# Keys of the streams and states of the matrix memory turned by VectorE from 128-byte pieces

## The chip, the cores and the metric

One core of one Trainium2 chip runs the whole kernel. The metric is the device time in microseconds, as the median of several runs. In the profile PE is TensorE, DVE VectorE, ACT ScalarE, POOL GpSimd and SP SyncE; PEld is TensorE's weight load, SPq the queue in which SP issues DMAs.

## The reference, cut to what matters

The kernel computes one layer for two groups of rows: 16 meta tokens with 256 new frames (the prompt), and 16 new frames of each of 8 running streams. One projection gives queries, keys and values of a differential attention (4 heads, two key halves of 128) and of an mLSTM matrix memory (4 heads), whose outputs are joined, projected, and followed by an MLP of 8192 columns. Two inputs have the wrong axis inside for TensorE: the cached keys and the stored states.

```python
def diff_attn_block(q, k, v, ...):            # k: cached keys of the last 256 frames, then the new ones
    s = jnp.einsum('bqhcd,bkhcd->bchqk', q, k) * (DQK_ATT ** -0.5) + bias
    p = jax.nn.softmax(s, axis=-1)
    w = p[:, 0] - lam * p[:, 1]
    o = jnp.einsum('bhqk,bkhd->bqhd', w, v)
    return rms_norm(o, subln_g) * (1.0 - lam_init)

def step(carry, blkin):                       # mLSTM, C: (streams, heads, 256, 128)
    num = einsum('bhts,bshe->bthe', A, vb) + iw * jnp.einsum('bhed,bthd->bthe', C, qb)
    ...
    C_new = dec * C + jnp.einsum('bhs,bshe,bshd->bhed', sw, vb, kb)
```

## The kernel before

All products are in float32. A weight matrix is read in pairs of tiles; a tile (2048 x 128, or 512 x 512 for the output projections) has four quarters. SP loads half a tile, 512 KB, at a time into one of four slots of raw (load_tile, load_rows, L462 and L469); ScalarE rounds a quarter to w_hi (split_hi, L481), VectorE takes the rest w_lo (split_lo, L490), and TensorE multiplies w_hi with the high and the low part of the activations and w_lo with the high part (mm_tile L510 to L512, mm_out L555 to L557). There are four buffers of split quarters; ScalarE waits until TensorE has done with the quarter four before. A slot of raw is loaded again when VectorE has split it.

The attention and the matrix memory are worked in beside these weight products. After every quarter each engine takes what is due from a list written out in advance: ATT_PLAN over tiles 24 to 41 (slot 0 is the first quarter of tile 24) and HEAD_PLAN over tiles 42 to 55. Each engine runs its items in order, between its own parts of the weight work, and waits on semaphores for what it needs from the others. TensorE takes slot n behind quarter n of the stage; VectorE takes slot n behind its split of the quarter four further on.

ATT_PLAN has 16 steps, the 8 streams and 8 blocks of the prompt in turn, one in four slots. For a stream the cached keys (256 frames x 1024, 1 MB) are loaded by POOL into kc, one buffer, when TensorE has turned those of the stream before. In slots -4 and -2 from the stream's scores TensorE transposes them with 16 products against the identity (turn, L1793) into PSUM, and ScalarE (L979) and VectorE (L1459) copy a half of each to kT, which has the feature in the partition and the frame inside. scores reads kT. In slot 1 of the stage VectorE also adds the mask to the bias (L1448).

HEAD_PLAN has 13 slots per head, the first head at slot 2: rows and decay at 0, scores, exponentials and weighted keys at 1, states at 2, weigh at 3, cn (products of the new state) at 4, take0 to take3 (new_state, L1603: decays C_rows and adds the products) from 4 to 6, num at 6, and then the norm, the gate and the turned output. The states of a head for all streams, 1 MB, are loaded by POOL into C_rows, which has the value's row in the partition (load_C). states turns them with 16 products into PSUM, and ScalarE copies them to C_T (L1064), which num reads. C_rows is then updated in place, stored by POOL as C_sample, and loaded with the next head.

Queues: SP issues the weight loads, and behind those of tile t the spill of tile t - 3 (the rows of mv and mo that the matrix memory needs later, L804), and from tile 50 on four loads of the residual (load_x, L811 and L812). POOL issues in one order: kc and vc of the streams; then mvo (the spilled rows; for one head it waits for that head's spills) and for each head the store of C_rows, the store of the prompt's state, the load of C_rows for the next head, and mvo of the head after that. ScalarE issues the stores of new keys (ko).

Of the kernel before, what the change touches and what calls it, by code (L numbers as in the profile page):

```python
# [19 lines left out]
P = 128  # L20
D = 2048
KT = D // P
# [38 lines left out]
T_OUT2 = 56  # L61
T_MLP = 64
# [54 lines left out]
KEYS_AT = (-4, -2)  # L117
# [3 lines left out]
HEAD_AT = (("rows", 0), ("decay", 0), ("scores", 1), ("expo", 1), ("ksw", 1), ("states", 2), ("weigh", 3), ("cn", 4),  # L121
           ("take0", 4), ("take1", 5), ("take2", 5), ("take3", 6), ("num", 6), ("hsum", 6), ("cp", 7), ("og", 7),
           ("hroot", 8), ("hturn", 11), ("gate", 11))
EXPO_LATE, EXPO_TAIL = 3 * P, 5 * P
DVX = DV + 2
# [80 lines left out]
def plan_banks():  # L206
# [20 lines left out]
    for _, what, n in ATT_PLAN:  # L227
        if what == "av":
            u.add(("av", n), (2, 4)[n % 2])
        elif what == "ko":  # L230
            u.add(("ko", n), 4)
        elif what == "keys":
            for i in range(2):
                u.add(("kT", n[0], 2 * n[1] + i), i)
        elif what == "scores":
            u.add(("s", STEPS[n], 0), 2)
            u.add(("s", STEPS[n], 1), 3)
        elif what == "turn":
            u.add(("w", STEPS[n]), 4)
        elif what == "out":  # L240
            u.add(("o", STEPS[n]), 5)
        elif what == "oturn":
            u.add(("oT", STEPS[n]), 1)
    u.add("nT", 1)
    for _, what, h in HEAD_PLAN:
# [7 lines left out]
        elif what == "states":  # L253
            for i in range(4):
                u.add(("ct", h, i), i % 3)
# [16 lines left out]
def build(nc, x_prompt, x_sample, cache_k, cache_v, state_C, state_n, state_m, meta_tokens, rel_bias, norm1_g,  # L272
# [6 lines left out]
    with ctx:  # L279
# [45 lines left out]
        ocol = sb("ocol", [P, 2, 6])  # L325
        n_sq = sb("n_sq", [P, 2, TOK])
        n_y = sb("n_y", [P, 2, TOK])
        n_t = sb("n_t", [P, TOK])
        g1 = sb("g1", [P, KT])
        g1_rows = sb("g1_rows", [KT, P])  # L330
# [30 lines left out]
        with ExitStack() as s:  # L361
            kc = sb("kc", [P, 2, ATTW], scope=s)
# [93 lines left out]
        def load_tile(e, pair, j, w, krow, col):  # L456
            for half in range(2):
# [4 lines left out]
                e.dma_start(raw[:, slot], w_source(w, krow + half * 8 * P, col)).then_inc(raw_landed[slot], 16)  # L462

        def load_rows(e, pair, j, w, krow, col):
            for half in range(2):
# [4 lines left out]
                            src.rearrange("(k p) n -> p k n", p=P)).then_inc(raw_landed[slot], 16)  # L470

# [156 lines left out]
        def _(e):  # L628
# [46 lines left out]
            dma(kc[:], cache_k[0, 0].rearrange("(a p) h n -> p a (h n)", p=P), "kc_in")  # L675
# [26 lines left out]
            for b in range(1, BD):  # L702
                done(e, ("kT", b - 1, 3))
                dma(kc[:], cache_k[0, b].rearrange("(a p) h n -> p a (h n)", p=P), "kc_in")
                if b >= 2:
                    done(e, ("o", b - 2))
                    dma(vc[:, b % 2], cache_v[0, b].rearrange("(a p) h n -> p a (h n)", p=P), f"vc_in{b % 2}")
# [72 lines left out]
        def _(e):  # L780
# [33 lines left out]

            for t in range(T_M, T_OUT):
                col = (N_MQ, N_MQ + 8 * P, N_MO)[(t - T_M) // 8] + P * ((t - T_M) % 8)
                load_tile(e, t // 2, t % 2, w_in[0], 0, col)
                spill(t - 3)
            for t in range(T_OUT, T_MLP):
                half, c = out_at(t)  # L820
                load_rows(e, t // 2, t % 2, w_out[0], (8 * half + 4 * (t % 2)) * P, 4 * c * P)
# [21 lines left out]
        def _(e):  # L843
# [108 lines left out]
            def att_work():  # L952

                for slot, what, n in ATT_PLAN:
                    yield slot
                    step = STEPS[n] if what in ("exp", "turn", *OUT_STEPS) else None
                    if what == "ko":

                        b = take(e, ("ko", n))
                        if n == 0:  # L960

                            e.wait_ge(S("kc_in"), 16)
# [11 lines left out]
                    elif what == "keys":  # L974
                        i = 2 * n[1]
                        k = take(e, ("kT", n[0], i))
                        if n[0]:
                            done(e, ("s", n[0] - 1, 1))
                        taken(e.activation(kT[:, 2 * i:2 * i + 2].rearrange("p c k -> p (c k)"), k[:], ACT.Copy),  # L979
                              ("kT", n[0], i))  # L980
# [55 lines left out]
            def head_work():  # L1036
                for slot, what, h in HEAD_PLAN:
                    yield slot
                    vo = None if what == "take" else mvo[:, h % 2]
# [21 lines left out]
                    elif what == "states":  # L1061
                        for i in range(4):
                            b = take(e, ("ct", h, i))
                            ins = e.activation(C_T[:, 2 * i:2 * i + 2, 0:DV], b[:].rearrange("p (s d) -> p s d", d=DV),  # L1064
                                               ACT.Copy)
                            taken(ins, ("ct", h, i))
# [67 lines left out]
            e.wait_ge(S("n_stored"), 32)  # L1134
            for t in range(T_OUT2, T_MLP):
# [46 lines left out]
        def _(e):  # L1182
# [253 lines left out]
            def att_work():  # L1436

                for slot, what, n in ATT_PLAN:
# [15 lines left out]
                    elif what == "keys":  # L1454
                        i = 2 * n[1] + 1
                        k = take(e, ("kT", n[0], i))
                        if n[0]:
                            done(e, ("s", n[0] - 1, 1))
                        taken(e.tensor_copy(kT[:, 2 * i:2 * i + 2].rearrange("p c k -> p (c k)"), k[:]),  # L1459
                              ("kT", n[0], i))  # L1460
# [135 lines left out]

            def new_state(h, i):

                b = take(e, ("cn", h, i))
                for half in range(2):  # L1600
# [35 lines left out]
            def head_work():  # L1636
                for slot, what, h in HEAD_PLAN:
                    yield slot
                    vo = None if what == "take" else mvo[:, h % 2]
# [23 lines left out]
                    elif what == "take":  # L1663
                        new_state(*h)
                    elif what == "cp":
# [118 lines left out]
        def _(e):  # L1784
# [163 lines left out]
            def att_work():  # L1948
                for slot, what, n in ATT_PLAN:
# [7 lines left out]
                    elif what == "keys":  # L1957
                        b, part = n
                        e.wait_ge(S("kc_in"), 16 * (b + 1))
                        for i in (2 * part, 2 * part + 1):  # L1960
                            turn(("kT", b, i), [(x * P, kc[:, x % 2, (2 * i + x // 2) * P:(2 * i + x // 2 + 1) * P])
                                                for x in range(4)])
# [16 lines left out]
            def numerators(h):  # L1979
                read_out(e, ("vn0", h), ("vn1", h), ("sx", h), ("sy", h), *[("ct", h, i) for i in range(4)])  # L1980
# [45 lines left out]
            def head_work():  # L2026
                for slot, what, h in HEAD_PLAN:
# [19 lines left out]
                    elif what == "states":  # L2047

                        e.wait_ge(S("C_in"), 32 * (h + 1))
                        for i in range(4):  # L2050
                            turn(("ct", h, i), [(x * P, C_rows[:, (4 * i + x) // 2, x % 2]) for x in range(4)])
# [135 lines left out]
```

## Time and profile before

| | |
|---|---|
| median of 3 runs | 1790.0 us (1789.85 to 1791.39) |
| the profiled execution | 1790.15 us, its span 1788.3 us |
| granted clock of TensorE | 1.00 |
| busy: PE, PEld | 1779.4, 1616.8 us |
| busy: DVE, ACT, POOL | 878.0, 694.5, 137.9 us |
| DMA | 251.42 MB, 141 GB/s in the mean |

The times in the profile are counted from the start of the span. The attention stage lies between about 243 and 465 us, the head stage between about 467 and 637 us. Products are pipelined: a row gives how long one product lasts, and the distance of two starts is what it costs in a sequence.

### The profile page before, as it was taken

The page shows a single profiled execution, that of the slowest core. Times are in us where ns is not written, and L with a number is a line of the kernel's source. Part 1 is how long each engine was busy: PE and PEld are TensorE (multiplying, and loading weights), DVE is VectorE, ACT ScalarE, POOL GpSimd, SP SyncE. Part 2 cuts the span into 40 slices and gives each one's busy share as a digit, 9 for nine tenths or more (in the row PEclk, how much of TensorE's full clock was granted, in tenths as well). Part 3 has the DMA queues.
Part 4 walks back from the last instruction along what each step waited for, and adds up shares of the span by engine and source line. Part 5 has one row for each costly group of instructions (what it writes and reads, how often), then busy time and mean ns, then how long its engine had stood idle before and what let it go on. Part 6 is the DMA issues. An engine that isn't in the chain of part 4 may idle for free.

```text
span 1788.3 us, 27850 instructions
## 1 busy us (share of the span) xinstructions
PE 1779.4 (100%) x9702; PEld 1616.8 (90%) x9702; DVE 878.0 (49%) x1678; ACT 694.5 (39%) x1320; POOL 137.9 (8%) x183
## 2 busy tenths in 40 slices
PE   9999999999999999999999999999999999999999
PEld 8999998999998888999888999888999888999887
DVE  5634774555566645555334444334445334445333
ACT  5324754544445444333323333323333332333332
POOL 3300000000111100111000111000111000111000
PEclk9999999999999999999999999999999999999999
DMA  7754456565666533444344444344443343443442
GB/s 193 224 142 108 107 156 207 149 193 144 192 183 222 159 120 120 119 125 128 121 128 129 119 127 123 125 129 126 120 129 119 127 129 121 125 126 120 147 147 95
DMA packets 297426, 251.42 MB, mean 141 GB/s; under 512 B 9340, under 2 KB 244156, under 8 KB 297356
## 3 DMA queue, kind: packets, MB, share of 16 engines
q1 hardware_dynamic: 281446, 209.50, 40.1%
q0 software_dynamic: 11088, 37.18, 6.2%
q10 hardware_dynamic: 4822, 3.80, 0.7%
q8 instruction: 46, 0.75, 0.2%
q14 instruction: 24, 0.20, 0.0%
HBM read 234.87 MB, written 15.56 MB: 140 GB/s over the span
## 4 chain that ended last, share of the span: by engine, by line
PE 97%; DVE 1%; DMA 1%; ACT 1%; issue 0%; POOL 0%; ACTq 0%; DVEq 0%
PE acc L510 18%; PE acc L511 17%; PE acc L512 17%; PE bank L597 8%; PE bank L598 8%; PE bank L596 8%; PE bank L1786 3%; PE ssb L596 2%; PE ssb L597 2%; PE ssb L598 2%; PE bank L1793 1%; PE ssb L1786 1%; PE bank L556 1%; PE bank L557 1%; PE bank L555 1%; PE acc L555 1%
## 5 line engine op out<-in xcount | busy, mean ns | idle before, releaser
L490 DVE TENSOR_TENSOR w_lo<-raw,w_hi 128x512 fp32r<-128x512 f32 x768 | 557.7, 734 | 829.0 <-ACT w_hi L481 828.3
L481 ACT ACTIVATE w_hi<-raw 128x512 fp32r<-128x512 f32 x768 | 482.7, 630 | 857.8 <-PE acc L512 425.0
L511 PE MATMUL acc<-x2g_lo,w_hi 128*128 128x384 f32 x1024 | 348.0, 340 | 0.0
L510 PE MATMUL acc<-x2g_hi,w_hi 128*128 128x384 f32 x1024 | 345.8, 338 | 0.0
L512 PE MATMUL acc<-x2g_hi,w_lo 128*128 128x384 f32 x1024 | 344.6, 337 | 0.0
L510 PE MATMUL acc<-a_hi,w_hi 128*128 128x400 f32 (+1 forms) x768 | 268.9, 350 | 0.2 <-DVE w_lo L490 0.2
L511 PE MATMUL acc<-a_lo,w_hi 128*128 128x400 f32 (+1 forms) x768 | 262.7, 342 | 0.0
L512 PE MATMUL acc<-a_hi,w_lo 128*128 128x400 f32 (+1 forms) x768 | 262.4, 342 | 0.0
L597 PE MATMUL bank<-w_lo,a_hi 128*128 128x512 f32 x640 | 253.0, 395 | 0.0
L598 PE MATMUL bank<-w_hi,a_lo 128*128 128x512 f32 x640 | 252.6, 395 | 0.0
L596 PE MATMUL bank<-w_hi,a_hi 128*128 128x512 f32 x640 | 252.0, 394 | 0.0
L512 PEld LDWEIGHTS acc<-x2g_hi,w_lo 128*128 128x128 f32 x1024 | 193.4, 189 | 0.0
L511 PEld LDWEIGHTS acc<-x2g_lo,w_hi 128*128 128x128 f32 x1024 | 192.3, 188 | 0.2
L510 PEld LDWEIGHTS acc<-x2g_hi,w_hi 128*128 128x128 f32 x1024 | 191.9, 187 | 0.5 <-DVE w_lo L490 0.3
L510 PEld LDWEIGHTS acc<-a_hi,w_hi 128*128 128x128 f32 x768 | 144.2, 188 | 3.1 <-issue 1.7
L598 PEld LDWEIGHTS bank<-w_hi,a_lo 128*128 128x128 f32 x640 | 120.7, 189 | 27.7
L597 PEld LDWEIGHTS bank<-w_lo,a_hi 128*128 128x128 f32 x640 | 120.3, 188 | 27.8
L596 PEld LDWEIGHTS bank<-w_hi,a_hi 128*128 128x128 f32 x640 | 120.4, 188 | 27.6
L512 PEld LDWEIGHTS acc<-a_hi,w_lo 128*128 128x128 f32 x768 | 144.7, 188 | 0.0
L511 PEld LDWEIGHTS acc<-a_lo,w_hi 128*128 128x128 f32 x768 | 144.4, 188 | 0.2
L762 POOL TENSOR_TENSOR a_lo<-n_sq,a_hi 128x384 f32 x64 | 64.9, 1015 | 959.8 <-ACT a_hi L1155 959.8
L1155 ACT ACTIVATE a_hi<-n_sq 128x384 f32 (+1 forms) x64 | 33.7, 526 | 131.9 <-DVE n_sq L1744 131.9
(340 smaller groups left out, 1529.0 us busy)
## 6 DMA issues: line engine op xcount, KB each, us to landing
raw<-in_w_up SPq DMA_DIRECT2D x128, 512.0 KB, 4.0
raw<-in_w_down SPq DMA_DIRECT2D x128, 512.0 KB, 3.9
raw<-in_w_in SPq DMA_DIRECT2D x94, 512.0 KB, 4.1
raw<-in_w_out SPq DMA_DIRECT2D x32, 512.0 KB, 3.9
kc<-in_cache_k POOLq DMA_DIRECT2D x8, 1024.0 KB, 6.6
vc<-in_cache_v POOLq DMA_DIRECT2D x8, 1024.0 KB, 9.1
C_rows<-in_state_C POOLq DMA_DIRECT2D x8, 512.0 KB, 8.0
out<-C_rows POOLq DMA_DIRECT2D x8, 512.0 KB, 5.2
```

The lines of the kernel that those rows point to most:

```text
L481: e.activation(w_hi[:, q], raw[:, slot, 4 * (q % 2):4 * (q % 2) + 4, :], ACT.Copy).then_inc(hi_ready, 1)
L490: e.tensor_tensor(w_lo[:, q], raw[:, slot, 4 * (q % 2):4 * (q % 2) + 4, :], w_hi[:, q].bitcast(F32), ALU.subtract).then_inc(lo_ready, 1)
L510: e.matmul(out, w_hi[:, q, kk], hi[:, k, at], start=k == 0, stop=False, skip_group_check=True)
L511: e.matmul(out, w_hi[:, q, kk], lo[:, k, at], start=False, stop=False, skip_group_check=True)
L512: last = e.matmul(out, w_lo[:, q, kk], hi[:, k, at], start=False, stop=k == KT - 1, skip_group_check=True)
L555: e.matmul(out, a_hi[:, k, rows], hi_w, start=k % 8 == 0, stop=False, skip_group_check=True)
L596: e.matmul(out, a_hi[:, k, rows], hi_w, start=k == 0, stop=False, skip_group_check=True)
L597: e.matmul(out, a_hi[:, k, rows], lo_w, start=False, stop=False, skip_group_check=True)
L598: last = e.matmul(out, a_lo[:, k, rows], hi_w, start=False, stop=k == KT - 1, skip_group_check=True)
L762: e.tensor_tensor(a_lo[:, bass.ds(2 * i + j, 1), LIVE], n_sq[:, j:j + 1, LIVE], a_hi[:, bass.ds(2 * i + j, 1), LIVE].bitcast(F32), ALU.sub ...
L1155: e.activation(a_hi[:, at, LIVE], n_sq[:, j:j + 1, LIVE], ACT.Copy).then_inc(S("u_hi_made"), 1)
L1786: return e.matmul(out, lhsT, rhs, start=start, stop=stop, skip_group_check=True)
```

## The change

The cached keys are no longer loaded by POOL as whole frames. SP loads them in four parts per stream into kc (now 128 x 4 x 512), each part with four DMAs of 32 partitions, whose pieces are 32 features (128 bytes): partition 32j + r holds the features 32j to 32j + 31 of frames 8r to 8r + 7. Parts 0 and 1 are issued behind the first half, parts 2 and 3 behind the second half of the weight loads of tiles 25, 27, ... 39. A part is loaded when the same part of the stream before has been turned. VectorE turns each part with one transpose of 128x512, which transposes every block of 32 x 32 and writes a frame's element 8 places behind the last, in slots -4, -3, -2 and -1 from the scores.

The states are loaded twice: by POOL into C_rows as before (now waited for by VectorE in take0), and by SP into a new buffer C_blk in 128-byte pieces, 4 parts of 8 DMAs per head, all 32 issued in one go behind the second half of the weight loads of tiles 41, 46, 49 and 52 (STATE_LOADS), ahead of that tile's spill. VectorE turns them with four such transposes per head, in slots -2, -1, 1 and 2 from the head's start, right into C_T. C_blk lies in the memory of n_sq, n_y and n_t, which are free in these stages.

The 192 transposing products of kc and C_rows, their banks and the copies L979, L1459 and L1064 are gone. POOL's loads of vc no longer have the loads of kc between them.

```diff
+STATE_LOADS = (41, 46, 49, 52)
-KEYS_AT = (-4, -2)
+BLOCKS_AT = (-4, -3, -2, -1)
+STATES_AT = (-2, -1, 1, 2)
...
-            plan += [(s + KEYS_AT[0], "keys", (step, 0)), (s + KEYS_AT[1], "keys", (step, 1))]
+            plan += [(s + at, "key_blocks", (step, i)) for i, at in enumerate(BLOCKS_AT)]
...
+        plan += [(s + at, "state_blocks", (h, i)) for i, at in enumerate(STATES_AT)]
...
+            def load_keys(b, i):
+                if b:
+                    e.wait_ge(S("blocks_turned"), 4 * (b - 1) + i + 1)
+                for j in range(4):
+                    e.dma_start(kc[32 * j:32 * j + 32, i].rearrange("p (x d) -> p x d", d=32),
+                                bass.AP(tensor=cache_k.tensor, offset=(b * PAST + 2 * i) * ATTW + 32 * j,
+                                        ap=[[8 * ATTW, 32], [P, 16], [1, 32]])).then_inc(S(f"kc_in{i}"), 16)
+            def load_states(h, i):
+                if h:
+                    e.wait_ge(S("states_turned"), 4 * (h - 1) + i + 1)
+                for x in range(2):
+                    for j in range(4):
+                        e.dma_start(C_blk[32 * j:32 * j + 32, i, x * DV:(x + 1) * DV].rearrange("p (a d) -> p a d", d=32),
+                                    bass.AP(tensor=state_C.tensor, offset=((2 * i + x) * NH + h) * DV * DQ + 32 * j,
+                                            ap=[[8 * DQ, 32], [DQ, 8], [1, 32]])).then_inc(S(f"C_blk_in{i}"), 16)
+            def behind_load(t):
+                if t in STATE_LOADS:
+                    h = STATE_LOADS.index(t)
+                    return lambda half: half and [load_states(h, i) for i in range(4)]
+                b, late = divmod(t - T_M - 1, 2)
+                if b in range(BD) and not late:
+                    return lambda half: [load_keys(b, 2 * half + i) for i in range(2)]
...
+                    elif what == "key_blocks":
+                        b, i = n
+                        e.wait_ge(S(f"kc_in{i}"), 64 * (b + 1))
+                        ...
+                        e.transpose(kT[:].rearrange("p c (r x) -> p x c r", x=8)[:, 2 * i:2 * i + 2],
+                                    kc[:, i].rearrange("p (x c d) -> p x c d", x=2, d=32)).then_inc(S("blocks_turned"), 1)
...
+            def state_blocks(h, i):
+                e.wait_ge(S(f"C_blk_in{i}"), 128 * (h + 1))
+                ...
+                e.transpose(C_T[:, 2 * i:2 * i + 2, 0:DV].rearrange("p b (r a) -> p b a r", a=8),
+                            C_blk[:, i].rearrange("p (b a d) -> p b a d", b=2, d=32)).then_inc(S("states_turned"), 1)
             def new_state(h, i):
                 b = take(e, ("cn", h, i))
+                if i == 0:
+                    e.wait_ge(S("C_in"), 32 * (h + 1))
...
             def scores(n, b):
                 if is_stream(b):
-                    read_out(e, *[("kT", b, i) for i in range(4)])
+                    e.wait_ge(S("blocks_turned"), 4 * b + 4)
```

## Rows read from the trace of the kernel before

**Rows 1.** The page, chain that ended last: shares of the span by engine.
```profile
PE 97%; DVE 1%; DMA 1%; ACT 1%; issue 0%; POOL 0%; ACTq 0%; DVEq 0%
```

**Rows 2.** Timeline of TensorE: start us, us, engine, line, operation, names, count [idle before].
```profile
244.93 1.04 PE L1793 MATMUL bank<-ident,kc 128*128 128x128 f32 x8
245.73 0.42 PE L510 MATMUL acc<-a_hi,w_hi 128*128 128x384 f32 x1
```

**Rows 3.** Timeline of TensorE: the two key groups that waited.
```profile
251.49 0.65 PE L1793 MATMUL bank<-ident,kc 128*128 128x128 f32 x4 [0.46 <-DVE kT L1459]
...
270.86 1.09 PE L1793 MATMUL bank<-ident,kc 128*128 128x128 f32 x8 [1.10 <-DMA kc<-in_cache_k]
```

**Rows 4.** Timeline of TensorE: the states of head 0.
```profile
480.58 2.08 PE L1793 MATMUL bank<-ident,C_rows 128*128 128x128 f32 x16
482.42 0.42 PE L510 MATMUL acc<-a_hi,w_hi 128*128 128x384 f32 x1
```

**Rows 5.** Instructions of kT, VectorE's copies: ns min/median/max, first and last start.
```profile
L1459 DVE COPY kT<-bank x16: 669/683/684, 250.8 to 431.4; 128x512 f32<-128x512 f32 x16
```

**Rows 6.** Stretches: us, then busy us (x) of PE, PEld, DVE, ACT, POOL, PEclk, DMA share, GB/s.
```profile
820.00:836.00 16.00, 16.00 (x92) 16.00 (x92) 8.51 (x12) 5.57 (x10) 2.03 (x2) 1.00 0.40 116
850.00:880.00 30.00, 30.00 (x131) 24.38 (x130) 10.49 (x17) 8.84 (x14) 0.00 (x0) 1.00 0.37 123
...
319.40:345.00 25.60, 25.60 (x194) 23.42 (x193) 12.95 (x41) 12.97 (x40) 1.39 (x2) 1.00 0.60 181
...
550.00:590.00 40.00, 39.48 (x225) 32.11 (x224) 27.00 (x79) 19.37 (x43) 5.67 (x7) 1.00 0.76 251
```

**Rows 7.** Timeline of VectorE at the start of the attention stage.
```profile
252.24 2.29 DVE L1448 TENSOR_TENSOR bias_p<-bias_p,s_sb 128x144 f32<-128x144 f32 x8
...
255.17 0.68 DVE L1459 COPY kT<-bank 128x512 f32<-128x512 f32 x1
...
256.37 0.55 DVE L1234 TENSOR_TENSOR m<-acc,rstd_x 128x384 f32<-128x384 f32 x1
```

**Rows 8.** Timeline of TensorE: first scores of stream 0.
```profile
256.75 0.66 PE L1786 MATMUL bank<-kT,zt 128*32 128x256 f32 x8
```

**Rows 9.** Timeline of VectorE: the splits around the weighing of head 0.
```profile
481.50 0.69 DVE L490 TENSOR_TENSOR w_lo<-raw,w_hi 128x512 fp32r<-128x512 f32 x1 [0.46 <-ACT w_hi L481]
485.52 0.69 DVE L490 TENSOR_TENSOR w_lo<-raw,w_hi 128x512 fp32r<-128x512 f32 x1 [3.32 <-ACT w_hi L481]
```

**Rows 10.** Timeline of SP's queue, tiles 46 and 47.
```profile
492.22 0.52 SPq L804 DMA_DIRECT2D mv_mo<-stage  x1
499.75 8.21 SPq L462 DMA_DIRECT2D raw<-in_w_in  x2
```

**Rows 11.** The page, DMA issues: engine, count, KB each, median us to landing.
```profile
raw<-in_w_in SPq DMA_DIRECT2D x94, 512.0 KB, 4.1
```

**Rows 12.** Instructions of mv_mo, the spills' issues: ns min/median/max, first and last start.
```profile
L804 SPq DMA_DIRECT2D mv_mo<-stage x16: 411/519/3384, 359.1 to 546.2; - x16
```

**Rows 13.** Timeline of ScalarE, VectorE and TensorE: when transfers and splits are wanted.
```profile
517.44 0.63 ACT L481 ACTIVATE w_hi<-raw 128x512 fp32r<-128x512 f32 x1 [1.43 <-PE acc L512]
...
528.65 1.11 DVE L1603 SCALAR_TENSOR_TENSOR C_rows<-C_rows,iwB,bank 128x128 f32<-128x128 f32 x4
...
549.04 1.29 DVE L490 TENSOR_TENSOR w_lo<-raw,w_hi 128x512 fp32r<-128x512 f32 x2 [1.79 <-ACT w_hi L481]
...
552.51 0.40 PE L555 MATMUL acc<-w_hi,a_hi 128*128 128x512 f32 x1
```

**Rows 14.** Timeline of POOL's DMA issues behind head 0.
```profile
497.80 0.70 POOL L630 DMA_DIRECT2D mvo<-mv_mo  x1 [17.37 <-issue]
498.49 1.80 POOL L630 DMA_DIRECT2D out<-C_rows  x2
...
507.94 1.77 POOL L630 DMA_DIRECT2D C_rows<-in_state_C  x2 [6.00 <-DMA out<-C_rows]
```

**Rows 15.** Instructions of C_rows: its products; its DMAs from issue to landing.
```profile
L1793 PE MATMUL bank<-ident,C_rows x64: 270/272/329, 480.6 to 603.2; 128*128 128x128 f32 x64
...
DMA to landing us min/median/max: 3.9/6.0/10.5
```

More of the change, by code:

```diff
@@ L325, in build @@
         ocol = sb("ocol", [P, 2, 6])
+        with ExitStack() as s:
+            C_blk = sb("C_blk", [P, 4, 2 * DV], scope=s)
         n_sq = sb("n_sq", [P, 2, TOK])
@@ L462, in load_tile, with load_rows @@
                 e.dma_start(raw[:, slot], w_source(w, krow + half * 8 * P, col)).then_inc(raw_landed[slot], 16)
-        def load_rows(e, pair, j, w, krow, col):
+                if behind:
+                    behind(half)
+        def load_rows(e, pair, j, w, krow, col, behind=None):
             for half in range(2):
@@ L470, in load_rows @@
                             src.rearrange("(k p) n -> p k n", p=P)).then_inc(raw_landed[slot], 16)
+                if behind:
+                    behind(half)
         def split_hi(e, pair, j, after=None):
@@ L701, in _ @@
             dma(vp[2 * P:NPR], av_rows[0:TAIL, 3], "v_stored")
[L702 to L707, printed above, removed]
+            for b in range(2, BD):
+                done(e, ("o", b - 2))
+                dma(vc[:, b % 2], cache_v[0, b].rearrange("(a p) h n -> p a (h n)", p=P), f"vc_in{b % 2}")
             e.wait_ge(S("w_made"), len(STEPS))
@@ L820, in _ @@
                 half, c = out_at(t)
-                load_rows(e, t // 2, t % 2, w_out[0], (8 * half + 4 * (t % 2)) * P, 4 * c * P)
+                load_rows(e, t // 2, t % 2, w_out[0], (8 * half + 4 * (t % 2)) * P, 4 * c * P, behind=behind_load(t))
                 spill(t - 3)
@@ L1038, in head_work @@
                     yield slot
-                    vo = None if what == "take" else mvo[:, h % 2]
+                    vo = None if what in ("take", "state_blocks") else mvo[:, h % 2]
                     if what == "rows":
@@ L1060, in head_work @@
                         last.then_inc(S("expo_exp"), 1)
[L1061 to L1066, printed above, removed]
                     elif what == "hsum":
@@ L1453, in att_work @@
                         e.wait_ge(S("lam_ready"), 1)
[L1454 to L1460, printed above, removed]
+                    elif what == "key_blocks":
+                        b, i = n
+                        e.wait_ge(S(f"kc_in{i}"), 64 * (b + 1))
+                        if i == 0 and b:
+                            done(e, ("s", b - 1, 1))
+                        elif i == 0:
+                            done(e, ("n", 7, 1))
+                        e.transpose(kT[:].rearrange("p c (r x) -> p x c r", x=8)[:, 2 * i:2 * i + 2],
+                                    kc[:, i].rearrange("p (x c d) -> p x c d", x=2, d=32)).then_inc(S("blocks_turned"), 1)
                     elif what == "scores":
@@ L1638, in head_work @@
                     yield slot
-                    vo = None if what == "take" else mvo[:, h % 2]
+                    vo = None if what in ("take", "state_blocks") else mvo[:, h % 2]
                     if what == "enter":
@@ L1664, in head_work @@
                         new_state(*h)
+                    elif what == "state_blocks":
+                        state_blocks(*h)
                     elif what == "cp":
@@ L1979, in numerators @@
             def numerators(h):
-                read_out(e, ("vn0", h), ("vn1", h), ("sx", h), ("sy", h), *[("ct", h, i) for i in range(4)])
+                read_out(e, ("vn0", h), ("vn1", h), ("sx", h), ("sy", h))
+                e.wait_ge(S("states_turned"), 4 * h + 4)
                 e.wait_ge(S("q_iw_made"), h + 1)
```

48 lines of the change are left out of this document (18 added, 30 removed).

## The prediction

> **What bounds the kernel now.** I read the chain that ended last first: TensorE holds 97% of it [rows 1]. With its granted clock at 1.00 in every stretch [rows 6], each microsecond of products taken off TensorE comes off the span, as long as nothing else becomes late. So the question is what is taken off TensorE, and what the new work (a VectorE instruction of a kind the trace doesn't hold, and small DMA pieces) makes late. The timeline around the removed products comes next [rows 2 to 4], then the table of stretches for how full the 16 DMA engines are [rows 6], VectorE's work at the start of the attention [rows 7 to 9], and last the queues of SP and POOL in the head stage, with the moments at which their transfers are wanted [rows 10 to 15].
>
> The sum is made against the profiled execution's 1790.15 us (span 1788.3); the median of the runs is 1790.0, so the same number holds for both.
>
> **What is removed.** Keys: 8 streams with two groups of 8 transposing products each. One group lasts from 244.93 to the next weight product at 245.73, 0.80 us [rows 2], so 16 x 0.80 = 12.8 us. Two groups also stood still: 0.46 us for a copy to kT, 1.10 us for the key DMA of stream 1 [rows 3]; together 14.4. States: a group of 16 runs from 480.58 to 482.42, 1.84 us [rows 4], four heads, 7.4 us. The first weight product behind such a group takes 0.42 us instead of 0.34 [rows 2, 4]; about 8 of the 20 groups stand between weight products only, 8 x 0.08 = 0.7 us. Removed: 14.4 + 7.4 + 0.7 = 22.5 us. The copies out of PSUM (ScalarE's for keys and states, VectorE's for half of the keys) go too; neither engine is on the chain, so that only helps the cover.
>
> **What VectorE gets.** 48 block transposes of 128x512, 32 for keys and 16 for states, against 16 copies of 0.68 us [rows 5]. Their duration is unknown. At the low end one pass over 512 elements as in that copy, 0.65 us; at the high end two passes, 1.35 us, because each element is written 32 bytes behind the last and no row shows a wide write of that kind. The nearest row is the 0.68, but its write is dense; I take the middle, 1.0 us, and keep both ends.
>
> In the steady attention stage this is covered: for 25.6 us of TensorE VectorE is busy 12.95 [rows 6]; it gets 4 x 1.0 and loses 2 x 0.68. A stream's last transpose comes right behind a weight split, and TensorE has a whole quarter of products (2.2 us) before its scores.
>
> Not so for stream 0. There VectorE also has the mask (2.3 us), and its rows from 252 to 256 us follow each other without idle time [rows 7]. Its last key block comes behind the copy that starts at 256.37 and lasts 0.55. Up to there it has one more transpose in slot 1, and two in place of copies in slots 0 and 2 (0.33 longer each), and then the fourth: 256.9 + 0.3 + 1.0 + 0.3 + 1.0 = 259.5. TensorE started the scores of stream 0 at 256.75 [rows 8]; without its two key groups (0.80 and 0.80 + 0.46, with 0.2 of gap) it comes at 254.5. It now waits 5.0 us (3.7 with 0.65 us, 6.4 with 1.35). What was hidden in TensorE's own transposes becomes a wait on VectorE; behind that wait are the scores and then every later product.
>
> In the head stage two of the four state transposes of a head (slots 1 and 2 behind the head's start) stand ahead of the weighing on which the new-state products wait. VectorE idled 0.46 and 3.32 us there [rows 9]; TensorE comes 1.9 us earlier, so 1.9 of 3.8 us remain against 2 x 1.0: 0.1 us late per head, 0.4 in all (0 with 0.65; 0.8 x 4 = 3.2 with 1.35).
>
> By the Trainium skill ("Vector Engine (DVE) Microarchitecture Reference", Measured stream behaviour on trn2) a port keeps its rate only for pairs of adjacent words, and a destination alone that steps 24 words every element costs 2.50 ns per column. Here the step is 8 words; at that figure a transpose would be an estimated 512 x 2.50 ns + 0.075 = 1.35 us, and the forecast would be the first rival's. No row of this kernel shows such a write.
>
> **What the DMA engines get.** A stream's keys are 8192 pieces of 128 bytes instead of 256 of 4 KB, a head's states 8192 more. Price of a piece: stretches that move only 512-byte rows show 116 GB/s at a share of 0.40, which is 512 B x 16 x 0.40 / 116 = 28 ns per piece and engine; 2 KB rows, 123 GB/s at 0.37, are 99 ns [rows 6]. The line through the two gives 11 ns at 128 bytes; in proportion to the bytes it is 7, as dear as a 512-byte piece 28. Between 7 and 28 I take 15, near the line. Room: a stream's period was 25.6 us with a share of 0.60, 15.4 us of all 16 engines, of which the old key load was 1 MB at the 2 KB rate (20.8 GB/s an engine), 3.1 us. The new period is 25.6 - 1.8 = 23.8, so 11.5 us are free, and the pieces take 512 per engine x 15 ns = 7.7 us. Hidden; so it stays up to 22 ns. The turned states of head 3 begin 122.6 us behind those of head 0 [rows 15], so a head has 41 us, now 39, at a share of at most 0.76 [rows 6]: 9 us free or more, for 7.7. Weights are queued behind the pieces, but one is issued at 499.75 for a split that begins at 517.44 [rows 10, 13], 17.7 us, and a load lands 4.1 us behind its issue [rows 11].
>
> **What SP and POOL get.** Key loads: 16 issues per stream, 0.5 us each (the median spill issue [rows 12]), 4 us between two weight loads that are two quarters apart: hidden. Head loads: 32 issues in a row, 16 us, and three things queue behind them on SP. The next weight load (before: 499.75) goes at 508.7 and lands by 513, before 517.44. The spill of a projected tile (before: 492.22) goes at 508.1 for head 1. POOL waits for it with mvo, which it issued 5.6 us behind the spill, and its queue goes on with the store of head 0's states and the load of head 1's, 10.1 us behind [rows 14]. So mvo goes at 513.7, the load at 523.8, and it lands 6.0 us (3.9 to 10.5 [rows 15]) behind its second issue, about 530.7. VectorE wants it at 528.65 - 1.9 = 526.8 [rows 13], where the change adds the wait that TensorE's removed transposes used to hold. It stands still 4 us, and with it the weight splits. Behind it are 1.8 us of idle [rows 13], and the tightest quarter later (the first split of the row at 549.04 ends at 549.7, taken 552.51 [rows 13]) has 2.8. Together that covers some 4; for what doesn't fit I put 0.5 us (0 to 6).
>
> **Sum.** 1790.15 - 22.5 + 5.0 + 0.4 + 0.5 = 1773.6 us. With transposes of 0.65 us it is 1790.15 - 22.5 + 3.7 + 0.5 = 1771.9.
>
> **Rivals.**
> 1. Strided writes: a transpose takes 1.35 us. Then 22.5 gained against 6.4 + 3.2 + 0.5: 1777.8. For it: the 32-byte step. Against: VectorE's ends hide it except at the two places named. Chance 0.17.
> 2. SP's queue: an issue takes 0.8 us when the queue is behind; the trace has a spill issue of 3.38 us [rows 12]. Then 32 issues are 25.6 us, the state load of head 1 lands at 540.3, VectorE waits 13.5, of which 4.0 are covered: 9.5 more on TensorE instead of 0.5, 1782.6. Against: 0.37 to 0.5 is usual. Chance 0.10.
> 3. A piece costs as much as a whole 512-byte one, 28 ns. Then a stream needs 14.3 us against 11.5, 2.8 x 8 = 22 us less the 10 or so that the prefetch holds: 12 lost, 1785.6. Chance 0.08.
> 4. The other side: a piece costs more than a 512-byte one. A break-even with before is reached when the streams lose the 16.6 us that the forecast gains, (0.512 c - 11.5) x 8 - 10 = 16.6, so c = 29 ns. At 56 ns (each piece paid twice) a stream needs 28.7 us, the streams lose 17.2 x 8 - 10 = 128 us, and the heads (28.7 - 12, between 9 and 15 free) x 4 = 67 more: some 1969 us. TensorE would wait for weight splits all through both stages. For it: no row has 98,000 such pieces. Against: the cost falls with the size from 2 KB to 512 bytes. Chance 0.15.
>
> The Trainium skill ("DMA: Bandwidth & Descriptors", Specifications) says that below 512 bytes a DMA does a read-modify-write, which speaks for rival 4; the trace can't show it.
>
> **Numbers.** The forecast has 0.50, with its own range 1768 to 1777 (less wait for stream 0's keys at the low end, dearer transposes at the high one). The range for 8 in 10 reaches over rivals 1 and 2 to 1784, and below to 1767. A measurement of this kernel tells 0.2% (3.6 us) from no change: below 1786.4 faster, above 1793.6 slower. Faster: 0.50 + 0.17 + 0.10 + 0.08 less 0.04 for the upper ends of rivals 2 and 3, which lie within 0.2%: 0.81. Slower 0.15, same 0.04.
>
> **What would show it.** Right: no transposing products of kc and C_rows; key and state transposes on VectorE near 1.0 us each; a wait of TensorE of some 5 us at the scores of stream 0 released by VectorE's key block and none for the later streams; VectorE waiting a few us for C_rows in head 1; a DMA share near 0.8 in the streams and weight splits that wait only for TensorE. Wrong: waits of ScalarE's splits for raw (pieces too dear, rivals 3 and 4), state issues on SP that last over 0.6 us each, or VectorE waiting for kc or C_blk.

## The result and the profile after

The changed kernel takes 1794.97 us in the median of 8 runs (1793.35 to 1797.31), the kernel before 1790.37 (1789.41 to 1791.39, 8 runs beside them): ratio 1.0026, 95% interval 1.0017 to 1.0035. It is slower by 4.6 us, where 16.5 less was forecast. The profiled execution took 1796.64 us with a span of 1794.8.

The page of the kernel after: busy time of each engine, the kinds of DMA packets, and the shares of the chain that ended last (against [rows 1]).
```profile
PE 1763.4 (98%) x9510; PEld 1599.5 (89%) x9510; DVE 914.4 (51%) x1710; ACT 677.8 (38%) x1288; POOL 132.3 (7%) x175
...
DMA packets 397650, 255.62 MB, mean 142 GB/s; under 512 B 111612, under 2 KB 346428, under 8 KB 397580
...
PE 89%; DMA 3%; DVE 3%; SPq 2%; issue 1%; ACT 1%; ACTq 0%; POOL 0%; DVEq 0%; POOLq 0%
```
TensorE fell from 97% to 89% of the chain, and SP's queue, which was not in it at all, holds 2%. So work left TensorE and waits came in its place. Where, is read from the start of the same weight product in both traces. Each line below is one product (t is the weight tile, q a quarter of it), in us from the span's start, after less before; three experiments, told further down, stand beside it. Each column is a single execution, and two of them are not typical: the one of the kernel after is 1.7 us above its median, that of e5 2.9 below.

```
product               before    after  diff | e5 diff  e3 diff  e9 diff
t24, start of stage   242.39   243.49  +1.10   +0.19    +0.08    +0.41
ahead of scores 0     254.10   252.75  -1.35   -2.26    -2.37    -2.04
4 quarters later      265.03   270.69  +5.66   +4.38    +5.24    -2.18
t40, behind stream 7  444.94   438.77  -6.17   -7.49    -6.57   -12.78
t44, behind head 0    490.11   484.74  -5.37   -7.37    -7.84   -13.79
t46 q3                524.55   517.30  -7.25   -9.25    -9.72   -15.67
t47 q2, in head 1     535.79   537.85  +2.06   -6.51    -9.69   -15.64
t52 q3                599.14   601.30  +2.16   -6.56   -10.59   -16.44
t54, behind head 3    616.86   623.04  +6.18   -3.04   -12.53   -18.40
```
The 1.10 at the start is no part of the change. From there TensorE gains 2.45 us up to the scores of stream 0, loses 7.0 at them, gains 11.8 in the streams, and loses 12.3 from head 0 on, where it should have gained. Three places hold the losses.

**Stream 0.** TensorE's timeline at its scores, against [rows 8], and VectorE's instructions in the same place, against [rows 7]:
```profile
254.85 0.60 PE L1929 MATMUL bank<-ident,m 128*128 128x128 f32 x4
260.82 1.11 PE L1824 MATMUL bank<-kT,zt 128*32 128x256 f32 x8 [5.37 <-issue]
```
```profile
253.81 2.29 DVE L1469 TENSOR_TENSOR bias_p<-bias_p,s_sb 128x144 f32<-128x144 f32 x8
256.13 1.10 DVE L1482 STREAM_TRANSPOSE kT<-kc 128x512 f32<-128x512 f32 x1
257.08 0.68 DVE L493 TENSOR_TENSOR w_lo<-raw,w_hi 128x512 fp32r<-128x512 f32 x1
257.67 1.07 DVE L1482 STREAM_TRANSPOSE kT<-kc 128x512 f32<-128x512 f32 x1
...
259.64 1.08 DVE L1482 STREAM_TRANSPOSE kT<-kc 128x512 f32<-128x512 f32 x1
```
The scores start 0.1 us behind the end of the fourth key block (259.64 + 1.08); the view names no releaser ("issue"), but nothing else ends there. The wait of 5.37 us costs 7.0, because TensorE comes out of it slowly. Stretches of the kernel after, columns as in [rows 6]: the idle one, and the next two.
```profile
254.80:260.80 6.00, 0.65 (x6) 0.33 (x5) 5.97 (x12) 0.63 (x1) 0.00 (x0) 0.73 0.93 177
260.80:263.40 2.60, 2.58 (x34) 1.87 (x35) 1.88 (x6) 0.00 (x0) 0.93 (x2) 0.50 1.06 248
263.40:266.00 2.60, 2.60 (x14) 2.60 (x14) 1.20 (x7) 1.12 (x4) 0.87 (x2) 0.80 1.15 332
```
The granted clock (PEclk) is 0.50, the 1.2 GHz level, in the 2.6 us behind the idle time, and 8 score products take 1.11 us instead of 0.66 [rows 8].

**The wait for C_rows in head 1.** The chain that ended last goes through SP's state issues, one after the other, and then through three DMAs (start us, us, what):
```profile
508.00 0.61 SPq L829
508.61 0.04 issue
508.65 2.26 DMA mv_mo<-stage
...
512.16 0.90 POOL out L633
513.06 10.63 DMA out<-C_rows
...
523.99 0.47 POOL C_rows L633
...
524.88 7.95 DMA C_rows<-in_state_C
...
532.92 1.12 DVE C_rows L1639 x4
```
SP's queue in the same stretch, against [rows 10], then VectorE and TensorE:
```profile
480.84 5.91 SPq L461 DMA_DIRECT2D raw<-in_w_in  x2
486.79 21.82 SPq L829 DMA_DIRECT2D C_blk<-in_state_C  x32
508.65 0.60 SPq L803 DMA_DIRECT2D mv_mo<-stage  x1
```
```profile
532.92 1.12 DVE L1639 SCALAR_TENSOR_TENSOR C_rows<-C_rows,iwB,bank 128x128 f32<-128x128 f32 x4 [11.29 <-DMA C_rows<-in_state_C]
```
```profile
534.10 2.52 PE L1824 MATMUL bank<-v_rows,expo 128*128 128x258 f32 x5 [6.74 <-DVE C_rows L1639]
```
VectorE stands still 11.29 us, TensorE 6.74 of them, and again it comes back slowly, with a granted clock of 0.54 in the 3.7 us behind:
```profile
534.10:537.80 3.70, 3.70 (x9) 2.94 (x10) 3.70 (x12) 0.00 (x0) 0.00 (x0) 0.54 0.33 46
```

**Weights behind the issues, heads 0 and 3 above all.** ScalarE's splits that waited for a weight load, and SP's queue ahead of the last of them (the line at 513.46 is head 1's):
```profile
456.58 0.63 ACT L484 ACTIVATE w_hi<-raw 128x512 fp32r<-128x512 f32 x1 [5.03 <-DMA raw<-in_w_in]
...
471.55 0.63 ACT L484 ACTIVATE w_hi<-raw 128x512 fp32r<-128x512 f32 x1 [5.73 <-DMA raw<-in_w_in]
...
513.46 0.64 ACT L484 ACTIVATE w_hi<-raw 128x512 fp32r<-128x512 f32 x1 [2.80 <-DMA raw<-in_w_in]
...
600.53 0.63 ACT L484 ACTIVATE w_hi<-raw 128x512 fp32r<-128x512 f32 x1 [7.62 <-DMA raw<-in_w_out]
```
```profile
569.92 22.82 SPq L829 DMA_DIRECT2D C_blk<-in_state_C  x32
592.78 0.60 SPq L810 DMA_DIRECT2D y_rows<-in_x_sample  x1
593.42 0.43 SPq L811 DMA_DIRECT2D y_rows<-in_x_prompt  x1
593.90 0.98 SPq L470 DMA_DIRECT2D raw<-in_w_out  x2
```
A late split makes VectorE late with the weighing behind it, and there TensorE waits, in head 3; behind this wait, too, its clock stood at 0.54:
```profile
612.32 1.88 PE L1824 MATMUL bank<-k_sw,v_rows 32*128 32x256 f32 x16 [4.40 <-DVE expo L1570]
```
```profile
612.30:616.00 3.70, 3.68 (x21) 2.66 (x22) 1.92 (x6) 0.00 (x0) 0.00 (x0) 0.54 0.68 221
```

### The profile page after: what moved, and what is told of

It reads as the page before. It is cut to its first block, busy times and chain, and to the rows that moved or that the text cites. A ratio compares the mean times of both kernels' runs of the same rounds, so it can differ in the third digit from the quotient of the medians.

```text
span 1794.8 us, 27669 instructions
## 1 busy us (share of the span) xinstructions
PE 1763.4 (98%) x9510; PEld 1599.5 (89%) x9510; DVE 914.4 (51%) x1710; ACT 677.8 (38%) x1288; POOL 132.3 (7%) x175
## 4 chain that ended last, share of the span: by engine, by line
PE 89%; DMA 3%; DVE 3%; SPq 2%; issue 1%; ACT 1%; ACTq 0%; POOL 0%; DVEq 0%; POOLq 0%
PE acc L513 16%; PE acc L514 16%; PE acc L515 16%; PE bank L600 8%; PE bank L601 8%; PE bank L599 8%; PE bank L1824 2%; SPq L829 2%; PE ssb L599 2%; PE ssb L600 2%; PE ssb L601 2%; PE ssb L1824 1%; PE bank L559 1%; PE bank L560 1%; PE bank L558 1%
```

## Experiments

All times are medians of 4 to 11 runs; the kernel before, on the same chips, took 1790.3 to 1790.9.

**e1, keys only**: the states as before, turned by TensorE out of C_rows.
```diff
-HEAD_AT = (("rows", 0), ("decay", 0), ("scores", 1), ("expo", 1), ("ksw", 1), ("weigh", 3), ("cn", 4),
+HEAD_AT = (("rows", 0), ("decay", 0), ("scores", 1), ("expo", 1), ("ksw", 1), ("states", 2), ("weigh", 3), ("cn", 4),
...
-        plan += [(s + at, "state_blocks", (h, i)) for i, at in enumerate(STATES_AT)]
...
```


> Only the keys are done the new way; the states are turned by TensorE out of C_rows as in the kernel before. Theory (SP's queue): the keys' part gains 14.4 us of products and stalls, loses 6.4 at the scores of stream 0 and some 0.5 in each of four streams: 1790.4 - 14.4 - 0.4 + 6.4 + 2.0 = 1784, between 1782 and 1787, faster. It is the states' part that costs. Rival (the transfers): if the 128-byte pieces of the keys are what costs, this kernel isn't faster, 1790 or more.

1784.64 us (1783.5 to 1784.88), ratio 0.9965 (0.9952 to 0.9979): the keys' part is a gain, of the size expected, though it holds all of the wait at stream 0.

**e2, states only**: the opposite, the keys as before.
```diff
-            plan += [(s + at, "key_blocks", (step, i)) for i, at in enumerate(BLOCKS_AT)]
+            plan += [(s + KEYS_AT[0], "keys", (step, 0)), (s + KEYS_AT[1], "keys", (step, 1))]
...
```


> Only the states are done the new way (loaded by SP in 32 issues in a row, turned by VectorE); the keys are turned by TensorE as before. Theory (SP's queue): TensorE's place against before fell by 12.3 us from the end of the streams to the end of the kernel, though 7.8 us of products went, so this kernel takes 1790.4 + 12.3 = 1802.7, between 1799 and 1805. Rival (the two parts only hurt each other, by a VectorE or DMA queue that is late from the streams on): the states alone gain or lose little, 1783 to 1793.

1801.04 us (1800.23 to 1802.25), ratio 1.0060 (1.0046 to 1.0073). The two parts add up: -5.7 and +10.7 make +5.0, against the 4.6 measured together. The loss is the states', and it does not need the keys.

**e3, state loads spread**: each weight half load is followed by one part (8 issues), over four of them; STATE_LOADS now counts half loads.
```diff
-STATE_LOADS = (41, 46, 49, 52)
+STATE_LOADS = (80, 92, 97, 103)
...
-                if t in STATE_LOADS:
-                    h = STATE_LOADS.index(t)
-                    return lambda half: half and [load_states(h, i) for i in range(4)]
+                parts = {at + i: (h, i) for h, at in enumerate(STATE_LOADS) for i in range(4)}
+                if 2 * t in parts or 2 * t + 1 in parts:
+                    return lambda half: 2 * t + half in parts and load_states(*parts[2 * t + half])
...
```


> As after, but a head's 32 state loads go in four lots of 8, one behind each of four weight loads, instead of 32 in a row. Pieces, bytes, issues and VectorE's transposes are the same. Theory (SP's queue): the 12.3 us lost from head 0 on go, and up to 7.8 us of removed products show: 1795.0 - 12.3 - 6 = 1777, between 1774 and 1782. Rival 1 (VectorE's 16 transposes of 1.16 us, two of each head ahead of the weighing): unchanged but for noise, 1792 to 1797. Rival 2 (the pieces fill the DMA engines): also unchanged, since all of them still move.

1777.96 us (1777.49 to 1778.99), ratio 0.9931 (0.9917 to 0.9944). SP's queue in head 1:
```profile
478.78 5.73 SPq L829 DMA_DIRECT2D C_blk<-in_state_C  x8
484.55 0.60 SPq L461 DMA_DIRECT2D raw<-in_w_in  x1
485.19 5.15 SPq L829 DMA_DIRECT2D C_blk<-in_state_C  x8
490.39 0.60 SPq L803 DMA_DIRECT2D mv_mo<-stage  x1
```
An issue costs the same as in the kernel after (median 0.61 us in both); what changed is what stands behind it. The spill goes at 490.39 instead of 508.65, and neither VectorE's wait for C_rows nor any split's wait for a weight is left in the heads. Pieces, bytes and transposes were all still there, so both rivals fall. The edit spreads the transfers in time together with their issues; that the issues' place is what counts, and not the bunched transfers, is shown for C_rows by e5. This one edit gives 17 us.

**e5, spill ahead of the issues**: the spill goes first in the four tiles, the weight load stays behind.
```diff
-                    return lambda half: half and [load_states(h, i) for i in range(4)]
+                    return lambda half: half and [spill(t - 3)] and [load_states(h, i) for i in range(4)]
...
-                spill(t - 3)
+                if t not in STATE_LOADS:
+                    spill(t - 3)
...
```


> As after, with one thing moved on SP: in the four tiles whose load is followed by 32 state loads, the spill of the projected tile goes ahead of these 32 instead of behind them. The weight load behind the 32 stays as late as in after. Theory (two separate chains behind SP's issues): only the chain spill, POOL's mvo, store of head 0's states, load of head 1's is freed, which cost 8.5 us in head 1 (VectorE's wait of 11.3 us for C_rows goes); the late weight loads of heads 0 and 3 still cost: 1795.0 - 8.5 = 1786.5, between 1785 and 1789. Rival (the wait for C_rows comes from the transfers and VectorE's load, not from the spill's place): 1793 to 1797.

1790.37 us (1787.46 to 1792.1), ratio 1.0000 (0.9991 to 1.0009): 4.6 us won, not 8.5, and outside the range expected. In its trace VectorE no longer waits for C_rows, and the losses behind late weights stay; SP and ScalarE in heads 1 and 3:
```profile
484.85 0.52 SPq L803 DMA_DIRECT2D mv_mo<-stage  x1
485.42 23.29 SPq L829 DMA_DIRECT2D C_blk<-in_state_C  x32
508.75 1.22 SPq L461 DMA_DIRECT2D raw<-in_w_in  x2
```
```profile
591.36 0.63 ACT L484 ACTIVATE w_hi<-raw 128x512 fp32r<-128x512 f32 x1 [7.17 <-DMA raw<-in_w_out]
```
So two chains run behind the issues, and the second also works in head 1 (2.7 us between t46 q3 and t47 q2 in the table; a split waited 4.82 us for its weights there, and TensorE 2.71 for the weighing behind it). The profiled run was the fastest of the eleven, 3 us under their median; what differs in the others no trace shows.

**e10, two lots of 16**, one behind each half load of the same tile.
```diff
-                    return lambda half: half and [load_states(h, i) for i in range(4)]
+                    return lambda half: [load_states(h, 2 * half + i) for i in range(2)]
```


> As after, but a head's 32 state loads go as 16 behind the first and 16 behind the second half load of the same weight tile. Theory (a load or spill may be late by its cover and no more): 16 issues hold SP for some 11 to 13 us, but the second lot still stands ahead of the spill, which is late by both lots, 22 us and more, so the wait for C_rows in head 1 stays (8.5 us), while the weight load between the lots is early and that behind is late by as much as in after: 1793 to 1796. Rival (only the length of one lot counts): 1779 to 1785.

1783.12 us (1782.56 to 1784.66), ratio 0.9961 (0.9948 to 0.9975): my expectation was wrong. SP's queue:
```profile
478.39 11.34 SPq L829 DMA_DIRECT2D C_blk<-in_state_C  x16
489.77 0.60 SPq L461 DMA_DIRECT2D raw<-in_w_in  x1
490.42 11.02 SPq L829 DMA_DIRECT2D C_blk<-in_state_C  x16
501.48 0.60 SPq L803 DMA_DIRECT2D mv_mo<-stage  x1
```
The spill does stand behind both lots, but the first lot now fills the time in which SP waited for the slot of the second half load (480.84 to 486.75 in the kernel after), so the spill goes 7 us earlier. VectorE's wait for C_rows was 5.7 us instead of 11.3, head 1 lost 3.9 at t47 q2, and the longest wait of a split for weights was 3.4. The time lies in the range of the rival, that only the length of one lot counts, so the time alone does not exclude it; against it stands that the spill went only when both lots, 22.4 us, were through. These rows fit a price that depends on how late each queued instruction is against its own cover; the number of issues alone, the same in the kernel after, e3, e5 and e10, does not give the four times.

**e7, dense writes**: the key transposes write their 512 elements side by side (the scores of the streams are then not the reference's).
```diff
-                        e.transpose(kT[:].rearrange("p c (r x) -> p x c r", x=8)[:, 2 * i:2 * i + 2],
-                                    kc[:, i].rearrange("p (x c d) -> p x c d", x=2, d=32)).then_inc(S("blocks_turned"), 1)
+                        e.transpose(kT[:, 2 * i:2 * i + 2].rearrange("p c (y d) -> p (c y) d", d=32),
+                                    kc[:, i].rearrange("p (y d) -> p y d", d=32)).then_inc(S("blocks_turned"), 1)
```


> As after, but the 32 key transposes write their 512 elements densely, 32 in a row, and not each 32 bytes behind the last; the keys stand in the wrong order in kT, so the scores of the streams are not the reference's. Read: the same 128x512. Theory 1 (the strided write is what lifts a transpose from the 0.68 us of a copy to 1.19): 0.60 to 0.75 us each; stream 0's wait falls by 4 x 0.5: 1793.0. Theory 2 (a transpose costs 1.19 us whatever it writes): 1.1 to 1.25 us and 1795.0.

The key transposes of the kernel after, and of this one (ns min/median/max, first and last start):
```profile
L1482 DVE STREAM_TRANSPOSE kT<-kc x32: 1070/1188/1251, 251.9 to 429.2; 128x512 f32<-128x512 f32 x32
```
```profile
L1482 DVE STREAM_TRANSPOSE kT<-kc x32: 689/703/712, 250.6 to 424.1; 128x512 f32<-128x512 f32 x32
```
The 32-byte step of the write is 0.49 of the 1.19 us; a dense transpose takes 0.70, about what a copy does (0.68) [rows 5]. The kernel takes 1791.22 us (1790.06 to 1793.53), ratio 1.0006 (0.9997 to 1.0015), 1.8 below what theory 1 gave.

**e4, all attention steps two quarters later**, stream 0's key blocks where they were.
```diff
-FIRST_PAIR, PER_PAIR, TILE_LATER = 4, 8, 4
+FIRST_PAIR, PER_PAIR, TILE_LATER = 6, 8, 4
...
-            plan += [(s + at, "key_blocks", (step, i)) for i, at in enumerate(BLOCKS_AT)]
+            plan += [(s + at - 2 * (n == 0), "key_blocks", (step, i)) for i, at in enumerate(BLOCKS_AT)]
```


> As after, but all attention steps come two quarters of a weight tile later, except the turning of stream 0's keys, which stays where it is. Theory: TensorE waits for VectorE's last key block because its scores come too early; two more quarters of weight products (2 x 2.2 us) stand before them, so 4.4 of the 6.4 us come back: 1790.6, between 1789 and 1792, and the wait at the scores of stream 0 is some 1.5 us. Rival (VectorE's backlog from the mask goes with it: the wait moves to a weight split or to the next step): 1794 to 1797, with the wait somewhere else.

1797.99 us (1796.5 to 1800.69), ratio 1.0046 (1.0033 to 1.0060), slower by 3.0 than the kernel after. At stream 0 it did what was expected (6.51 us from weight product to weight product there, of which 2.2 are a quarter and 1.6 the scores, so 2.7 of loss instead of 7.0; 1.95 of it is a wait for VectorE's copy of av_rows, not for the key block), but the last steps of the attention are held to the stage's last slot and now fall together. The rival's mechanism was the right one, with a time 1 us above its range: the wait went to the end, and the clock fell to 0.50 behind it.
```profile
464.01 0.69 PE L1831 MATMUL bank<-ident,o_rows 128*128 128x128 f32 x2 [2.99 <-ACT o_rows L1040]
```

**e6, the mask behind the key blocks** of stream 0.
```diff
-    plan = [(1, "mask", 0)]
...
+        if n == 0:
+            plan.append((s - 1, "mask", 0))
```


> As after, but VectorE makes the mask of the scores (2.3 us) behind the fourth key block of stream 0, not between the first and the second. Theory (TensorE waits for VectorE's queue at stream 0): the key blocks are ready 2.3 us earlier, TensorE waits 4.1 instead of 6.4 us, and the softmax, which gets the mask late, has cover: 1795.0 - 2.3 = 1792.7, between 1791.5 and 1794. Rival (the mask's lateness comes back through the softmax and the weights' transposes): 1794 to 1797.

1791.17 us (1789.95 to 1792.97), ratio 1.0004 (0.9995 to 1.0013): 3.8 us won, more than the mask's 2.3, since the last key block is ready at 257.27 (260.72 in the kernel after, whose stage began 0.9 later) and behind the shorter wait, 2.78 us, the granted clock stayed at 1.00.

**e8, everything spread**: e3 and e6, and the steps of stream 0 alone two quarters later. Beside the lines of e3:
```diff
+        if n == 0:
+            plan.append((s - 1, "mask", 0))
+            s += 2
```


> The state loads in four lots of 8 (as the run with spread states, 1778.0), the mask behind the key blocks of stream 0, and the scores of stream 0 (with its later steps, of this stream alone) two quarters of a weight tile later, the key blocks where they were. Theory: 4.4 us of weight products and 2.3 us of earlier key blocks cover the 6.4 us wait: 1778.0 - 6.2 = 1771.8, between 1770 and 1774. Rival (the steps of stream 0 then run into those of the prompt's first step and VectorE is late there, as where all steps were later): 1775 to 1779.

1774.71 us (1774.07 to 1775.7), ratio 0.9913 (0.9900 to 0.9927): half of the 6.2 us expected on top of e3. The key blocks were in time; the mask now stood ahead of VectorE's copy of av_rows, and TensorE, which takes the bank that this copy frees, waited there:
```profile
261.80 0.63 PE L1931 MATMUL bank<-ident,zt 128*128 128x128 f32 x4 [2.68 <-DVE av_rows L1402]
```

**e9, the mask two slots later**, behind that copy, on e8.
```diff
-            plan.append((s - 1, "mask", 0))
+            plan.append((s + 1, "mask", 0))
```


> As the run with everything spread (1774.7), but the mask goes one more VectorE slot later, behind the AV copy of that slot. There the key blocks were no longer late, but VectorE's mask stood ahead of the AV copy, and TensorE waited 2.7 us for the bank that this copy frees (its turning of the K rows). Theory: that wait goes and nothing takes its place: 1774.7 - 2.6 = 1772.1, between 1771 and 1773.5. Rival (the mask delays the softmax of stream 0 instead): 1774 to 1776.

(The move is of two slots, from 3 to 5; "one more slot" above was a slip.) 1772.22 us (1771.78 to 1772.49), ratio 0.9897 (0.9882 to 0.9912), 18.6 us faster than before and 22.8 than the change. Its chain, and TensorE at stream 0 without a wait:
```profile
PE 96%; DVE 2%; ACT 1%; issue 1%; ACTq 0%; POOL 0%; DVEq 0%; POOLq 0%
```
```profile
258.95 0.63 PE L1931 MATMUL bank<-ident,zt 128*128 128x128 f32 x4
259.51 0.66 PE L1826 MATMUL bank<-kT,zt 128*32 128x256 f32 x8
```

**e11, key blocks of streams 1 to 7 a slot earlier**, on e9.
```diff
-            plan += [(s + at, "key_blocks", (step, i)) for i, at in enumerate(BLOCKS_AT)]
+            plan += [(s + at - (n > 0), "key_blocks", (step, i)) for i, at in enumerate(BLOCKS_AT)]
```


> As the run before it in this list (mask one slot later), but the key blocks of streams 1 to 7 are turned one VectorE slot earlier. Theory: from stream 1 on TensorE never waits for a key block, so it is the same, 1771 to 1773.5. Rival (the 0.4 to 0.8 us that TensorE still loses at the scores of streams 1 to 3 is a wait for the last key block): 1.5 us faster, 1770.5.

1772.40 us (1771.9 to 1773.2), ratio 0.9898 (0.9883 to 0.9913): the same. No later stream waits for its key blocks; what TensorE still loses at the scores of streams 1 to 3 stays open.

## Why the prediction was wrong

**The step that failed is "What SP and POOL get"**: "Head loads: 32 issues in a row, 16 us". They take 21.8 to 25.9 us. Most issues of such a row last 0.61 us with 0.04 between two, a few of them 1.2 to 2.2, so an issue costs 0.68 to 0.81 us in the mean of a lot; I had taken the 0.5 of a lone spill's median [rows 12]. The term of the sum for all that queues behind them was 0.5 us. It measured 9.3 in head 1, 6.0 at the products behind the weighing of head 3 and 1.5 at those of head 0, some 17 in all, and 17 is what e3 gives back. Rival 2 named this mechanism with 0.8, at a chance of 0.10. But the price alone does not give the result; the same step had more wrong:

- The chain to C_rows was stretched by more than the issues. I had VectorE waiting 4 us. The issues added 5.8; mvo went 2.8 behind the spill instead of 5.6 (-2.8); the load of C_rows went 12.5 instead of 10.1 behind mvo (+2.4), since the store ahead of it took 10.63 us to land; and the load took 8.9 from issue to use, not 6.9 (+2.0). Together 11.4, and 11.3 were measured. My landing time of 530.7 looks close to the real 532.8 only because I had left SP's start where it was before, while the whole stage came 5 to 7 us earlier: moments of the trace before must be moved together, or only differences used.
- "Together that covers some 4" held: 11.3 of wait left 6.7 for TensorE. But behind the wait its clock stood at 0.54, which I had not priced; TensorE lost 9.3 us there, 0.8 of it at the weighing.
- "The next weight load goes at 508.7 and lands by 513, before 517.44" left a margin of 4.6 us, and 5.8 to 9.9 more for the issues take it. I looked at this queue for head 1 alone. In head 3 two loads of x stand between the issues and the weights. In head 0 a weight load issued at 455.37 took 16.2 us to land. The same load took 4.5 in the kernel before, where it went at 457.66 in a stage 6.2 us later, so here it was issued 3.9 us late. No state piece moved any more then, but four held-up half loads went within 3.2 us, and POOL's loads for the head stage from 454.8 on. e5 keeps these losses with the wait for C_rows gone, e3 is without both.

**Point by point.** Removed, 22.5: not refuted; e9 gains 18.8 us on TensorE from the start of the stage (from +0.41 to -18.40), and the rest is some 0.9 us lost at the start of head 0 (in e1 and in e2 too, so either part brings it by itself; why stays open), 0.8 in head 2, and small waits at the scores. Transposes: forecast 1.0 us, measured 1.19 for keys and 1.16 for states, between the two. By the Trainium skill ("Vector Engine (DVE) Microarchitecture Reference", Measured stream behaviour on trn2) the estimate was 1.35. The trace agrees in direction, a strided destination costs, but the size here is 1.19 against 0.70 dense (e7). Stream 0: forecast 5.0, the wait was 5.4 and the loss 7.0, the clock again. Weighing: forecast 0.1 in each head from the idle time of head 0. In e3 three heads lose nothing there, but in head 2 TensorE waits 1.45 us for VectorE's weighing instead of 0.52 and loses 0.8, so the 0.4 in all was half of what it costs. Pieces: this was right. A stream's period in the kernel after, against the 0.60 of [rows 6]:
```profile
349.41:373.07 23.66, 23.66 (x175) 21.52 (x173) 15.93 (x41) 11.15 (x33) 0.38 (x2) 1.00 0.78 177
```
0.78 x 23.66 is 18.5 us of all 16 engines; before it was 0.60 x 25.6 = 15.4, of which 3.1 for the old load. So 6.2 us for 512 pieces an engine, 12 ns a piece (forecast 15, bounds 7 to 28). Rivals 3 and 4 are refuted: a piece of 128 bytes is cheaper than one of 512 (28 ns). The Trainium skill ("DMA: Bandwidth & Descriptors", Specifications) says that a DMA does a read-modify-write below 512 bytes. For these loads no price of it shows beyond that of a small piece, which costs less by the piece and more by the byte (128 bytes in 12 ns against 512 in 28).

Two of the signs of being wrong appeared: state issues of 0.61 us, over 0.6, and splits that waited for raw. The second I had put down to dear pieces; e3 moves the same pieces and has no such wait, so this sign didn't tell pieces from queue.

The outcome was on the slower side, but not by the mechanism that I had put there. Rival 2's mechanism, worked through all four heads and with the clock behind each wait, would have come nearest; its own number, 1782.6, was a gain of 7.5 us where 4.6 were lost.

## What to carry to other kernels

Many small DMAs cost first on the queue that issues them, 0.68 to 0.81 us each here in rows of 32, and what they hold up is everything queued behind them: list it for every place where the lot is issued, with its own cover, and spread the lot so that each wait is within its cover (17 us here for the same transfers; fewer and larger issues, or another engine's queue, were not tried). A long wait of TensorE is dearer than its length: behind 4.4 to 6.7 us of idle time its products ran at about half clock for some 3 us. When a stage moves earlier, shift every moment read from the old trace by the same amount, and when work is taken off a bound engine, look for what the new order puts ahead of the one copy that frees its next bank.

## What the runs showed of the hardware

- Issue time on SP does not follow the number of pieces or bytes. The two groups of the kernel after, 512 pieces each (keys) and 256 (states), and the weights' half loads, 512 KB each:
```profile
L819 SPq DMA_DIRECT2D kc<-in_cache_k x128: 311/578/1630, 233.1 to 413.4; - x128
```
```profile
L829 SPq DMA_DIRECT2D C_blk<-in_state_C x128: 572/608/2217, 429.2 to 592.1; - x128
```
```profile
L461 SPq DMA_DIRECT2D raw<-in_w_in x94: 367/373/6081, 8.3 to 509.8; - x94
```
  A lone weight issue takes 0.37 us. Right behind a row of others a spill took 0.60 and a weight load 0.43 to 0.68. What makes an issue in a row dearer than a lone one no run shows.
- The transpose of 128x512 on VectorE: 0.70 us with a dense write, 1.19 with a step of 32 bytes, with the same read.
- TensorE's granted clock fell to its 1.2 GHz level (0.50 to 0.54) behind idle times of 4.4, 5.4 and 6.7 us in the kernel after and of 3.0 in e4, and stayed at 1.00 behind 2.7 in e5 and e8 and 2.8 in e6. At the low level eight score products took 1.11 us instead of 0.66. The mean clock of the span tells it: 0.995 in the kernel after, 1.000 before and in e9.
